# The rotary part of latent-attention scores as two rounded products, on one Trainium2 core

## The reference, cut to what matters

```
q_rope = apply_rope(q_rope, cos[:, :, None, :], sin[:, :, None, :])
k_rope = apply_rope(k_rope, cos, sin)
...
s = (jnp.einsum('bqhd,bkhd->bhqk', qn, k_nope).astype(jnp.float32)
     + jnp.einsum('bqhr,bkr->bhqk', qr, k_rope).astype(jnp.float32)) * scale
```

## Time and profile before

| what | value |
|---|---|
| median of 3 runs | 2531.89 us (2531.88 to 2533.27) |
| the profiled execution's own time | 2532.84 us |
| its span, first to last instruction | 2531.1 us |
| PE busy | 2517.0 us (99%) |
| DVE busy | 1851.9 us (73%) |
| ACT busy | 1313.4 us (52%) |
| POOL busy | 25.5 us (1%) |

### The profile page before, as it was taken

How to read it: one execution, slowest core, us unless ns; L and a number is a source line. 1 busy time by engine, 2 the same in 40 slices (tenths; PEclk the granted TensorE clock), 3 DMA queues, 4 the chain that set the end, 5 groups by cost and what they waited for, 6 DMA issues and landing times.

```text
span 2531.1 us, 33093 instructions
## 1 busy us (share of the span) xinstructions
PE 2517.0 (99%) x12088; PEld 2110.2 (83%) x12088; DVE 1851.9 (73%) x2983; ACT 1313.4 (52%) x1885; POOL 25.5 (1%) x24
## 2 busy tenths in 40 slices
PE   8999999999999999999999999999999999999999
PEld 6888888888888888888888887888888888888888
DVE  8777658777658777677777786678777767777766
ACT  6665565565566444444444555765544444444443
POOL 4000000000000000000000000000000000000000
PEclk9999999999999999999999999999999999999999
DMA  7554556554555555555555554444555555555554
GB/s 302 202 191 171 198 185 234 169 193 168 199 184 189 193 198 186 196 184 201 197 191 183 190 202 151 148 158 173 186 199 190 192 184 198 200 196 188 197 183 150
DMA packets 71231, 480.84 MB, mean 190 GB/s; under 512 B 8000, under 2 KB 10688, under 8 KB 17216
## 3 DMA queue, kind: packets, MB, share of 16 engines
q1 hardware_dynamic: 71104, 479.16, 53.6%
HBM read 475.72 MB, written 2.10 MB: 189 GB/s over the span
## 4 chain that ended last, share of the span: by engine, by line
PE 83%; DVE 1%; ACT 1%; issue 0%; ACTq 0%; DVEq 0%
PE acc L942 12%; PE acc L944 12%; PE acc L943 12%; PE score L942 10%; PE score L944 10%; PE score L943 10%; PE acc L928 9%; PE acc L932 4%; PE score L1281 1%; PE score L928 1%; PE head_ps L1306 0%; PE score L932 0%; PE turn_ps L1290 0%; DVE low L1777 0%; PE head_ps L1307 0%
## 5 line engine op out<-in xcount | busy, mean ns | idle before, releaser
L1777 DVE TENSOR_TENSOR low<-raw,high 128x1024 fp32r<-128x1024 f32 (+2 forms) x912 | 1079.2, 1188 | 468.6 <-ACT high L1370 460.5
L1370 ACT ACTIVATE high<-raw 128x1024 fp32r<-128x1024 f32 (+2 forms) x912 | 935.0, 1028 | 846.9 <-PE acc L944 436.3
L928 PE MATMUL acc<-xs,high 128*128 128x512 f32 x1184 | 396.8, 398 | 1.5 <-DVE xs L2312 1.3
L942 PE MATMUL acc<-high,xs 128*128 128x512 f32 x928 | 366.3, 395 | 0.3 <-DVE scale_a L1870 0.3
L944 PE MATMUL acc<-low,xs 128*128 128x512 f32 x928 | 361.6, 390 | 0.0
L943 PE MATMUL acc<-high,xs 128*128 128x512 f32 x928 | 361.1, 389 | 0.0
L932 PE MATMUL acc<-xs,low 128*128 128x256 f32 x1184 | 297.6, 279 | 0.0
L942 PE MATMUL score<-high,xs 128*128 128x512 f32 x736 | 286.4, 389 | 0.0
L944 PE MATMUL score<-low,xs 128*128 128x512 f32 x736 | 286.3, 389 | 0.0
L943 PE MATMUL score<-high,xs 128*128 128x512 f32 x736 | 286.3, 389 | 0.0
L928 PEld LDWEIGHTS acc<-xs,high 128*128 128x128 f32 x1184 | 219.4, 188 | 50.2 <-DVE xs L2312 2.0
(11 more groups left out here) (398 smaller groups left out, 3177.1 us busy)
## 6 DMA issues: line engine op xcount, KB each, us to landing
raw<-w_up_dram SPq DMA_DIRECT2D x176, 1024.0 KB, 4.8
raw<-w_in_dram SPq DMA_DIRECT2D x76, 1024.0 KB, 4.8
raw<-w_wide_dram SPq DMA_DIRECT2D x75, 1024.0 KB, 4.8
raw<-w_out_dram SPq DMA_DIRECT2D x32, 1024.0 KB, 4.8
raw<-w_heads_dram SPq DMA_DIRECT2D x20, 1024.0 KB, 4.8
raw<-w_mixout_dram SPq DMA_DIRECT2D x16, 1024.0 KB, 4.8
raw<-w_mem_dram SPq DMA_DIRECT2D x8, 1024.0 KB, 4.8
raw<-w_first_dram SPq DMA_DIRECT2D x8, 1024.0 KB, 4.8
```

Of the source, the lines that this page charges most:

```text
L928: return eng.matmul(bank_, hi, moving, start=start, stop=False)
L942: eng.matmul(bank_, xh, hi, start=start, stop=False)
L1370: eng.activation(high[:, s % SPLIT, to:to + n * P], raw[:, s % RAW, at_:at_ + n * P], ACT.Copy).then_inc((highs_a, highs_b)[piece], 1)
L1777: eng.tensor_tensor(low[:, s % SPLIT, w], raw[:, s % RAW, at_:at_ + n * P], high[:, s % SPLIT, w].bitcast(F32), ALU.subtract).then_inc((lo ...
```

## The change

- The rotary part of the scores is no longer one full float32 product of `q` and `kr` but two float32r products with one stationary operand, which stacks the rounded queries of a head in 64 partitions and their rounded remainder in the other 64. The first moves `key_high` (the rounded key in all 128 partitions), the second `key_low` (its remainder, beside the rounded queries only, zeros elsewhere).
- `rope_q` moves from slot 23 to slot 21.
- ACT rounds heads 0 to 3 into `rope_first` in slot 22, and heads 4 to 7 into `rope_late` in slot 24 (64 x 1024 values each). DVE makes the remainder of the first in slot 22, GpSimd that of the second.
- The scores wait for `rope_low` or `rope_pool` instead of `roped`.
- `rope_k` has two more operations on 128 x 256 values: one addition over all partitions and a rounding copy; its last two become subtractions.
- `gate`, which nothing used, gives its place to `key_high`. `rope_first` lies over `memk`, `rope_late` over the last third of `lats`.
- The parameter work ahead of slot 23 of layer 0 moves to the start of `out1`.

```diff
-    put(23, "rope_q", layer)
+    put(21, "rope_q", layer)
+    put(22, "rope_split", layer, 0)
+    put(24, "rope_split", layer, 1)
...
+        rope_first = at("rope_first", [P, HEADS // 2, S], F32R, cursor[0] - 4 * S * MEM)
...
-        kr = at("kr", [P, 2, S], F32, work + 44 * KB)
+        key_low = at("key_low", [P, 2, S], F32R, work + 44 * KB)
+        rope_late = at("rope_late", [P, HEADS // 2, S], F32R, work + 16 * KB)
...
-                qk = [(q[:, h, :], kn[:, h, :]), (q[:, HEADS + h % 4, :], kr[:, h // 4, :])]
+                rope = (rope_first, rope_late)[h // 4][:, h % 4, :]
+                qk = [(q[:, h, :], kn[:, h, :]), (rope, key_high[:, :]), (rope, key_low[:, h // 4, :])]
...
-                        eng.wait_ge(roped, 2 * layer + 2)
+                        eng.wait_ge((rope_low, rope_pool)[h // 4], layer + 1)
...
+                elif kind == "rope_split":
+                    layer, half = a
+                    eng.wait_ge(roped, 2 * layer + 2)
+                    to = (rope_first, rope_late)[half]
+                    a_ = slice(ROPE * half, ROPE * half + ROPE)
+                    eng.activation(to[a_, :, :], q[a_, HEADS:, :], ACT.Copy).then_inc(rope_high, 1)
...
+            for layer in range(DEPTH):
+                eng.wait_ge(rope_high, 2 * layer + 2)
+                eng.tensor_tensor(rope_late[0:ROPE, :, :], q[ROPE:, HEADS:, :], rope_late[ROPE:, :, :].bitcast(F32), ALU.subtract)\
+                    .then_inc(rope_pool, 1)
...
+                    step_(eng.tensor_tensor(lat[:, 6, :], lat[:, 6, :], lat[:, 7, :], ALU.add))
+                    step_(eng.tensor_copy(key_high[:, :], lat[:, 6, :]))
                     for half in range(2):
                         a = slice(ROPE * half, ROPE * half + ROPE)
-                        ins = eng.tensor_tensor(kr[a, half, :], lat[a, 6, :], lat[a, 7, :], ALU.add)
+                        ins = eng.tensor_tensor(key_low[a, half, :], lat[a, 6, :], key_high[a, :].bitcast(F32), ALU.subtract)
...
+                elif kind == "rope_split":
+                    layer, half = a
+                    if half == 0:
+                        eng.wait_ge(rope_high, 2 * layer + 1)
+                        eng.tensor_tensor(rope_first[ROPE:, :, :], q[0:ROPE, HEADS:, :], rope_first[0:ROPE, :, :].bitcast(F32), ALU.subtract)\
+                            .then_inc(rope_low, 1)
...
-                if name == "in_b0":
+                if name == "out1":
```

More of the change, by code:

```diff
@@ L418, in build @@
         wide_turn = at("wide_turn", [P, WIDE_TILES, S], F32, memh_at)
-        gate = at("gate", [P, S], F32)
+        key_high = at("key_high", [P, S], F32R)
         silu_g = at("silu_g", [P, S], F32)
@@ L512, in build @@
         swapped, kr_swapped = sem("swapped"), sem("kr_swapped")
-        roped = sem("roped")
+        roped, rope_high, rope_low, rope_pool = sem("roped"), sem("rope_high"), sem("rope_low"), sem("rope_pool")
         gated = sem("gated")
@@ L2097, in do @@
                         a_ = slice(ROPE * (1 - half), ROPE * (1 - half) + ROPE)
-                        ins = eng.memset(kr[a_, half, :], 0.0)
+                        ins = eng.memset(key_low[a_, half, :].bitcast(F32), 0.0)
                     step_(ins)
```

## The result

| | before | changed |
|---|---|---|
| median of 20 runs each | 2532.28 us (2531.8 to 2533.27) | 2535.87 us (2533.97 to 2537.68) |
| the profiled execution's own time | 2532.84 | 2534.06 |
| its span | 2531.1 | 2532.3 |

The account below looks back on a forecast made before the run. PE was taken as the bound, busy 2517.0 of 2531.1 us. Waits of 4.7 us minus 3.2 saved by the products gave 1.5 slower, 2533.4 us on the median of 2531.89; range 2530.5 to 2538.0.

Parts of the forecast that it names:

- The products: New rotary products in the scores take 0.46 us a head against 0.66, 3.2 us saved over 8 heads in 2 layers.
- The rival of a slow narrow product: A 128-column rounded product takes 0.23 us like the full one, so 0.6 us is lost, time 2537.2; chance 24%.
- The 81 ns of the Trainium skill: Documented pace of a sustained 128-column product, weight load included; would save 1.0 us more, 4.2; not used in the forecast.
- The wait: PE waits ahead of `in_b` behind DVE's earlier rotation, 2.34 us and 2.31 us in the two layers, 4.7 us lost.
- The swapped transfers: The four transfers SP issues for the rotation land by 134.3 at the latest, before DVE reaches `rope_q` in slot 21.
- The sum: Whole kernel: 4.7 us lost minus 3.2 saved, 1.5 us slower; 2533.4 us on the median.
- its own case: Both the saving and PE's delay ahead of `in_b` come as priced: 2531.5 to 2535.5 us; chance 60%.
- The clock: Rival: PE's clock falls behind the new pause ahead of `in_b`, up to 3.2 us a layer, time 2539.8; chance 8%.
- "a clock under 1.00 behind the gap": Listed sign of a wrong forecast: PE's granted clock below 1.00 after its gap ahead of `in_b`; expected to stay 1.00.
- What lay beside other work: ACT's roundings, GpSimd's subtraction, `rope_k`'s 0.8 us and the parameter work run beside PE's work and cost it nothing.
- GpSimd's subtraction: Second remainder takes about 5.3 us, four DVE splits each 0.25 longer; hidden by DVE's idle time, at worst 2 x 1 us.
- The parameter work was booked at nothing in its new place: 1.19 us of DVE work moved to `out1` costs nothing beside idle DVE, 1 us at most if that cover fails.

## Why the prediction came out as it did

**The products** were priced right. 1.11 us for a head's scores in place of 1.31, in every trace; the 128-column product is at 0.11 (148.83 to 148.94), the lower bound that was taken, and the kernel without the key's remainder shows the same price in time. The rival of a slow narrow product is out. The 81 ns of the Trainium skill (TensorE: Matmul & The Clock Gate, Back-to-back issue gap), which would have made the saving 1.0 larger, did not appear either. In time less than the 3.2 us came in: 4.7 - 1.8 = 2.9 in the lowest group of this kernel, and 2.4 with the rotation one slab sooner. The forecast has no term for what is missing. Pairs of products behind head 3's scores became 2% longer, 0.3 us over both layers, and with the rotation one slab sooner GpSimd's hold on DVE cost PE 0.24 us more.

**The wait** came where and as long as worked out: 2.36 us against 2.34 in layer 0, released by the store of `v_mla`, with the rotation just ahead. The swapped transfers were there in time. 4.7 us for both is what the rotation alone cost in its lowest group (2536.7 against 2532.0).

**The sum** of +1.5 describes the runs in which nothing else happened: the fastest four are 1.8 us above the median of before. It does not describe the median, +3.6, and 2535.87 also lies above the 2531.5 to 2535.5 that the forecast gave to its own case.

**The clock** is the step that was wrong, in its form and its chance. I had made it a rival of 8% that decides from one point on and costs up to 3.2 us a layer. The runs show something between: behind a wait of this length the clock falls in some waits and not in others, here in 23 of 40 by the groups, and a fall costs 1.7 us. So 23 x 1.7 us, spread over 20 runs, is 2.0 us on average, and 1.8 + 2.0 = 3.8 is the mean's distance, near the median's 3.6. The forecast's own sign of being wrong, "a clock under 1.00 behind the gap", fits the 16 of the 20 runs whose mean clock is 0.999. That the median is inside the stated range is partly luck: falls in both layers at the price assumed would have given 2539.8, outside it. The place and the sign of the mechanism were right, its price was taken from the start of the kernel, twice too high, and it should have been a term of the sum with a share, not a case by itself.

**What lay beside other work.** ACT's rounding in slot 24 and `rope_k` cost nothing that the trace shows; no wait of PE was added at slots 24 to 30. GpSimd's subtraction was expected at 5.3 us with four splits each 0.25 longer. It took 2.4, and in layer 0 a single DVE operation beside it bore it all:

```profile
150.84 2.40 POOL L1779 TENSOR_TENSOR rope_late<-q,rope_late 64x1024 fp32r<-64x1024 f32 x1 [110.69 <-ACT rope_late L1656]
```

```profile
151.95 2.38 DVE L1792 TENSOR_TENSOR low<-raw,high 128x1024 fp32r<-128x1024 f32 x1
```

1.2 us more on DVE, near the 1 us foreseen, and hidden as foreseen in this kernel. With the rotation one slab sooner it was 2.2 us in layer 0 and not wholly hidden. The parameter work was booked at nothing in its new place, which holds; that it left a place of value shows only when the rotation is in slot 22.

## What to carry to other kernels

Where one engine has no idle time left, look at a moved step from its queue: what stands behind it there, and when the full engine wants that. Here a step of 3.8 us moved ahead of one that had 1.4 us to spare (3.77 - 2.36); the same gain without the wait was one slot further on. And a wait of over 2 us on a busy TensorE costs more than its length, because the clock may fall behind it: many times of the same kernel show it as groups, a single profile does not.

## What was not expected of the hardware

- Behind a pause of TensorE of 2.1 us in the profile the granted clock fell to 0.50 in 43 of 78 cases, counted by the groups of times, and in the traces stayed there for about 3.4 us. One such fall cost 1.7 us. Behind pauses of 0.8 us it fell in 0 of 22 cases; behind 3.3 us in both that were traced, once for 3.4 us and once for 6.9.
- While GpSimd subtracted 64 x 1024 values (2.4 us), a DVE operation with two inputs in SBUF, the core's main buffer, that started meanwhile was held until GpSimd was done, in all 14 cases of the seven traces that have this subtraction. It ended behind GpSimd's end by somewhat less than its own length alone: 1.09 us for a split of 1.22, 0.28 for one of 0.42. One with an input from the products' banks (`branch`, 0.42 us) was not held. In layer 1 of the changed kernel it was one of 2 columns, 0.16 us alone, and it ended with GpSimd's at 532.0:

```profile
529.64 2.40 POOL L1779 TENSOR_TENSOR rope_late<-q,rope_late 64x1024 fp32r<-64x1024 f32 x1 [376.40 <-ACT rope_late L1656]
```

```profile
529.82 2.24 DVE L2171 TENSOR_TENSOR scale_b<-scale_b,par 128x2 f32<-128x2 f32 x1
```

In the changed kernel it cost no time, because DVE had idle time left; with the rotation one slab sooner it cost PE 0.24 us. The Trainium skill (GPSIMD Engine Reference, Key points) has the contention; the numbers are these traces'.

- Pairs of rounded products were 2% longer (0.353 against 0.347 us) over some 10 us in each layer, behind head 3's scores, once both new products were in the scores. The cause was not found.
